# A Mamba-2 (SSD) mixer stage, reordered: the next group's projections stand between this group's heads, VectorE works on whole rows of chunks, and ScalarE and GpSimd split the weights

## The chip, the core and the metric

The kernel runs on one core of one Trainium2 chip. A core has five engines that run side by side and meet only at semaphores: TensorE (PE; its weight loads are listed apart as PEld), VectorE (DVE), ScalarE (ACT), GpSimd (POOL) and SyncE (SP), which here starts the DMAs. The metric is the device time of one execution in microseconds (us). Matmuls read SBUF and write PSUM (8 banks of 512 floats in each of 128 partitions).

## The reference

Two layers of a diffusion backbone run over 640 tokens: 512 latent tokens and 128 context tokens. Layer 0 mixes tokens with a bidirectional Mamba-2 scan, layer 1 with gated DeltaNet, and each is followed by an expert-retrieval mixer. The change touches the Mamba-2 mixer alone:

```python
proj = h @ w_in                                  # z, xbc, dt
xbc  = silu(short_conv(xbc, conv_w) + conv_b)    # 3 taps along the tokens
dt   = softplus(dt_raw + dt_bias);  a = -exp(a_log)
acs  = cumsum(dt * a)                            # inside a chunk
lmat = exp(where(tril, acs[i] - acs[j], -inf))   # decay matrix of a head
cb   = einsum('bcign,bcjgn->bcijg', cm, bm)      # C_i . B_j, one per group
y_in = einsum(cb * lmat, x * dt)                 # inside a chunk
y_x  = einsum(c, state) * exp(acs)               # from the states before it
s    = s * exp(acs[-1]) + einsum(b, xdt * exp(acs[-1] - acs))
y    = rmsnorm((y_f + y_b + xs * d_skip) * silu(z)) @ w_out
```

There are 4 groups of 8 heads; each head has 64 channels and a state of 128; every step is done forward and backward. The reference has chunks of 64 tokens, the kernel takes chunks of 128, so 4 latent chunks and 1 of context.

## The kernel before

Activations lie features-first: 128 features in the partitions, 640 tokens along the row. The stage in question is `ssd_groups_phase` (line 600), which loops over the 4 groups. A group has ten weight tiles of 128 columns: four of x, one of B, one of C (these six go through the conv) and four of z, the gate. Projections are fp32 in three passes: the weight and the input are each split into a high and a low part, and `project` (L673, matmuls at L187) does high x high, high x low and low x high, 48 matmuls of 320 columns for a tile. A weight tile lands in one buffer `w` (L666); VectorE rounds it to the high part (L339) and subtracts to get the low part (L341); TensorE waits for both.

Within a group the work goes in three steps:

- Conv tiles: TensorE projects six tiles in a row, ScalarE takes the middle tap (L756) and the SiLU (L760), VectorE adds the two outer taps out of PSUM (L427).
- States: TensorE turns x and B to tokens-first (L689) and makes `cb` (L695). VectorE weighs the tokens (L824), TensorE makes the eight state increments one by one (L703), and VectorE carries the states from chunk to chunk (L842, L847).
- Heads: for head r, `sums` (L712) makes the cumulated decay of both directions in PSUM. VectorE takes the difference with a mask added, chunk by chunk (L858), ScalarE takes two exponentials (L772, L773), VectorE multiplies by C (L887), by dt, adds the directions and multiplies by `cb` (L890, L895, L899), and TensorE multiplies the result `m` with the tokens and `ea` with the states (L735, L738). Every second head a z tile is projected first, and `heads_out` (L866, L871) writes two heads.

Each engine takes its instructions in the written order, and semaphores carry what one engine owes another. PSUM is four slots of two banks; a table (`order`, L609) says who uses which slot next. The loop over groups is one body, run four times: a group's first projection stands behind the last head of the group before, and VectorE lets the next group begin (`group_free`, L903) when its last output is written. TensorE's order inside the heads is these lines:

```python
for r in range(SR):
    if r + 1 < SR:
        sums(r + 1)
    ...
    if r % 2 == 0:
        project(SCONV + q)
        slots.claim(pe, ("y", q), i)
    ...
    pe.wait_ge(m_ready, SR * i + r + 1)
```

Of the kernel before, what the change touches and what calls it, by code (L numbers as in the profile page):

```python
# [16 lines left out]
ALU = mybir.AluOpType  # L17
# [416 lines left out]

def out_projection_phase(k, name, w_dram, src, tiles, layer):
# [164 lines left out]
def ssd_groups_phase(k, parts, stats, y):  # L600

    nc, d = k.nc, k.dram
    NW = 2
    assert STILES % NW == 0 and SXT > NW + 1
    FWD, BWD = 0, 1


    incs = [(FWD, 0), (BWD, 3), (FWD, 1), (BWD, 2), (FWD, 2), (BWD, 1), (FWD, CTXC), (BWD, CTXC)]
    order = [(("proj", t), t % 4) for t in range(SCONV)]  # L609
    order += [(("turn", c), (SCONV + c) % 4) for c in range(NC)]  # L610
    order += [("cb", 3)] + [(("inc", n), 2 + n % 2) for n in range(len(incs))]
    order += [((what, r), slot) for r in range(SR) for what, slot in (("sumf", 0), ("sumb", 1))]

    order += [((what, n + q), 2 + q % 2) for q in range(SXT) for what, n in (("proj", SCONV), ("y", 0))]
    with ExitStack() as ctx:
# [4 lines left out]
        convw_all, convw = sb("convw_all", [P, SG, SCONV, 4]), sb("convw", [P, SCONV, 4])  # L620
        skip_all, skip = sb("skip_all", [P, SG, SXT]), sb("skip", [P, SXT])
        st = sb("stats", [P, 5, NC, 2, SR])
        xbc = sb("xbc", [P, SCONV, T])
        tok = sb("tok", [P, NC, (SXT + 1) * P])
        cb = sb("cb", [P, T])
        state = sb("state", [P, 2, NC - 1, SXT * P])
        lm = sb("lm", [P, 2, 2, T])
        ea = sb("ea", [P, 2, 2, T])
        m = sb("m", [P, 2, T])

        tap = m
        xw = ea[:, 0].rearrange("p d t -> p (d t)")[:, 0:2 * SXT * P].rearrange("p (b n) -> p b n", b=2)
        decayed = ea[:, 1].rearrange("p d t -> p (d t)")[:, 0:SXT * P]
        ctx_state = lm[:, 1].rearrange("p d t -> p (d t)")[:, 0:2 * SXT * P].rearrange("p (b n) -> p b n", b=2)
        ysum = sb("ysum", [P, T])
        B, C = xbc[:, SXT], xbc[:, SXT + 1]

        small, w_loaded, w_split = sem("small_loaded"), sem("w_loaded"), sem("w_split")
        init_loaded, group_free, stat_ready = sem("init_loaded"), sem("group_free"), sem("stat_ready")
        centre, tapped, convolved, gated = sem("centre_ready"), sem("tapped"), sem("convolved"), sem("z_ready")  # L640
        turned, cb_ready = sem("turned"), sem("cb_ready")
        weighted, states_ready, ctx_ready, ctx_stored = (sem(s) for s in (
            "weighted", "states_ready", "ctx_ready", "ctx_stored"))
        diff, lm_ready, m_ready, m_used = sem("diff_ready"), sem("lm_ready"), sem("m_ready"), sem("m_used")
        ps = k.ps
        block = ctx.enter_context(nc.Block())

        @block.sync
        def _(sp):
            sp.dma_start(convw_all[:], d["ssd_conv"]).then_inc(small, 16)  # L650
            sp.dma_start(skip_all[:], d["ssd_skip"]).then_inc(small, 16)
            with sp.Fori(0, SG) as i:
                for t in range(STILES):
                    if t == SCONV:
                        sp.wait_ge(group_free, i + 1)
                        for dr, first in ((FWD, 0), (BWD, NC - 2)):
                            sp.dma_start(state[:, dr, first], d["ssd_state"][bass.ds(2 * i + dr, 1)]
                                         .rearrange("o n p -> n (o p)")).then_inc(init_loaded, 16)
                    if t == SCONV + NW + 1:

                        for dr in range(2):
                            sp.wait_ge(ctx_ready, 2 * i + dr + 1)
                            sp.dma_start(d["ssd_out"][bass.ds(2 * i + dr, 1)].rearrange("o n p -> n (o p)"),
                                         ctx_state[:, dr]).then_inc(ctx_stored, 16)
                    sp.wait_ge(w_split, STILES * i + t + 1)
                    sp.dma_start(w[:], d["ssd_w_in"][bass.ds(STILES * i + t, 1)]  # L666
                                 .rearrange("o p k n -> p (o k) n")).then_inc(w_loaded, 16)
            sp.wait_ge(ctx_stored, 32 * SG)

        @block.tensor  # L670
        def _(pe):
            with pe.Fori(0, SG) as i:
                def project(t):  # L673
                    pe.wait_ge(w_split, STILES * i + t + 2)
                    slots.claim(pe, ("proj", t), i)
                    s = slots.slot(("proj", t))
                    for kt in range(KT):
                        last = three_passes(nc, ps[:, s], (whi[:, t % NW, kt], wlo[:, t % NW, kt]),
                                            (parts[0][:, kt], parts[1][:, kt]), kt == 0, kt == KT - 1)
                    last.then_inc(slots.ready[s], 1)  # L680

                for t in range(SCONV):
                    project(t)
                pe.wait_ge(convolved, SCONV * (i + 1))
                for c in range(NC):
                    slots.claim(pe, ("turn", c), i)
                    s = slots.slot(("turn", c))
                    for t in range(SXT + 1):
                        last = nc.tensor.transpose(ps[:, s, t * P:(t + 1) * P], xbc[:, t, c * P:(c + 1) * P],  # L689
                                                   k.c("ident"))  # L690
# [1472 lines left out]
```

## Time and profile before

| | us |
|---|---|
| median of 3 runs | 6237.69 (6228.37 to 6243.76) |
| the profiled execution's own time | 6234.22 |
| its span in the trace | 6232.4 |
| the stage: first weight DMA issued to last VectorE end | 217.85 to 1051.26 |

Over the whole span the page gives

```profile
PE 4920.7 (79%) x27154; PEld 4314.5 (69%) x27154; DVE 4364.5 (70%) x7749; ACT 1670.4 (27%) x2016; POOL 1605.7 (26%) x1060
```

That is an average over stages with different limits. The page's map cuts the span into 40 slices of 156 us; the stage is in the second to seventh:

```profile
PE   6677676854689999997777777777854589999997
POOL 0000000011026667773000000000011016666774
PEclk7788888877569999998888988899977559999999
```

[...] In the stage TensorE is busy six to seven tenths at some eight tenths of its clock, and GpSimd does nothing. A wait is read as: who waited, who released it, how long.

### The profile page before, as it was taken

Reading aid. Unit: us, or ns where it says so; the run is one execution under the profiler, and the core shown is the slowest. Engines: PE = TensorE matmul, PEld = TensorE weight load, DVE = VectorE, ACT = ScalarE, POOL = GpSimd, SP = SyncE. Lnnn points to the kernel's source line nnn. Section 1 sums busy time; section 2 is a strip of 40 time slices with the busy share of each in tenths; the row PEclk is TensorE's granted clock in tenths of the full one; section 3 lists DMA queues with packets and bytes.
Section 4 is the critical chain, followed back from the end, with each engine's and each line's share of the span. In section 5 each row is a group of like instructions: output and inputs, shape, how many; then the busy total and the mean of one; then the engine's idle time right before and its main releaser. Section 6 shows DMA issues by size and latency. Waiting matters only on the chain. (4 is left out here: it accounts for less than half of the span.)

```text
span 6232.4 us, 77006 instructions
## 1 busy us (share of the span) xinstructions
PE 4920.7 (79%) x27154; PEld 4314.5 (69%) x27154; DVE 4364.5 (70%) x7749; ACT 1670.4 (27%) x2016; POOL 1605.7 (26%) x1060
## 2 busy tenths in 40 slices
PE   6677676854689999997777777777854589999997
PEld 2566665754469888996766666666844359988896
DVE  1555554379759999998455555565279759999997
ACT  0122222211343333332212211121211243333332
POOL 0000000011026667773000000000011016666774
PEclk7788888877569999998888988899977559999999
DMA  8100110110159999995000000000110159999996
GB/s 359 40 28 21 38 38 4 54 38 23 71 234 402 401 401 397 397 398 209 29 25 25 25 25 21 16 18 21 54 38 23 54 217 401 401 402 398 397 395 261
DMA packets 340323, 1059.27 MB, mean 170 GB/s; under 512 B 28272, under 2 KB 135024, under 8 KB 316656
## 3 DMA queue, kind: packets, MB, share of 16 engines
q1 hardware_dynamic: 192624, 519.24, 22.0%
q0 software_dynamic: 147456, 536.94, 21.9%
q8 instruction: 135, 2.21, 0.2%
q14 instruction: 108, 0.88, 0.0%
HBM read 998.92 MB, written 57.15 MB: 169 GB/s over the span
## 5 line engine op out<-in xcount | busy, mean ns | idle before, releaser
L1836 POOL DMA_INDIRECT dense_ring<-in_peer_u_rows,dense_eid x512 | 723.3, 1413 | 934.6 <-DVEq L1952 583.8
L1608 POOL TENSOR_TENSOR top_w_lo<-top_w,top_w_hi 128x1024 fp32r<-128x1024 f32 x32 | 96.1, 3021 | 3342.4 <-ACTq L1576 3342.4
L1836 POOL DMA_INDIRECT dense_ring<-in_peer_v_rows,dense_eid x512 | 786.1, 1535 | 290.6 <-DVE dense_acc L1993 189.0
L1850 PE MATMUL psum<-peer_in_hi,dense_u_hi 128*128 128x384 f32 x2048 | 690.1, 337 | 44.8 <-DVE dense_u_lo L1958 44.8
L1850 PE MATMUL psum<-peer_in_hi,dense_u_lo 128*128 128x384 f32 x2048 | 690.4, 337 | 0.0
L1850 PE MATMUL psum<-peer_in_lo,dense_u_hi 128*128 128x384 f32 x2048 | 688.8, 336 | 0.0
L1993 DVE SCALAR_TENSOR_TENSOR dense_acc<-dense_ring,dense_weight,dense_acc 128x1024 f32<-128x1024 f32 x508 | 640.0, 1280 | 0.0
L1861 PE MATMUL psum<-dense_v_hi,dense_a_hi 128*128 128x512 f32 x1536 | 604.5, 394 | 18.7 <-DVE dense_a_lo L1972 17.1
L1985 DVE SCALAR_TENSOR_TENSOR dense_ring<-dense_ring,peer_rows 128x1024 f32<-128x1024 f32 x512 | 614.7, 1219 | 0.0
L1861 PE MATMUL psum<-dense_v_hi,dense_a_lo 128*128 128x512 f32 x1536 | 603.5, 393 | 0.0
L1861 PE MATMUL psum<-dense_v_lo,dense_a_hi 128*128 128x512 f32 x1536 | 602.8, 392 | 0.0
L1850 PEld LDWEIGHTS psum<-peer_in_hi,dense_u_hi 128*128 128x128 f32 x2048 | 386.6, 189 | 55.5 <-DVE dense_u_lo L1958 45.7
L1916 ACT CAST dense_a_hi<-dense_gelu 128x384 fp32r<-128x384 f32 x256 | 131.7, 515 | 1058.8 <-DVE dense_gelu L1967 1058.8
L1977 DVE TENSOR_TENSOR dense_v_lo<-dense_v,dense_v_hi 128x1024 fp32r<-128x1024 f32 x256 | 312.6, 1221 | 127.2 <-ACT dense_v_hi L1911 127.0
L1850 PEld LDWEIGHTS psum<-peer_in_lo,dense_u_hi 128*128 128x128 f32 x2048 | 386.2, 189 | 9.8
L1850 PEld LDWEIGHTS psum<-peer_in_hi,dense_u_lo 128*128 128x128 f32 x2048 | 385.9, 188 | 0.0
L1861 PEld LDWEIGHTS psum<-dense_v_hi,dense_a_hi 128*128 128x128 f32 x1536 | 289.2, 188 | 89.1 <-issue 23.9
L1911 ACT CAST dense_v_hi<-dense_v 128x1024 fp32r<-128x1024 f32 x256 | 268.4, 1048 | 277.0 <-DMA dense_v<-in_peer_v_rows 276.7
L1713 PE MATMUL psum<-gate_high,gate_second 128*128 128x128 f16 x768 | 324.8, 423 | 17.0 <-DVEq L1768 17.0
L1861 PEld LDWEIGHTS psum<-dense_v_hi,dense_a_lo 128*128 128x128 f32 x1536 | 288.7, 188 | 61.1
L1861 PEld LDWEIGHTS psum<-dense_v_lo,dense_a_hi 128*128 128x128 f32 x1536 | 288.9, 188 | 54.4
L1714 PE MATMUL psum<-gate_low,gate_second 128*128 128x128 f16 x768 | 324.2, 422 | 0.0
(339 smaller groups left out, 10170.4 us busy)
## 6 DMA issues: line engine op xcount, KB each, us to landing
dense_u<-in_peer_u SPq DMA_DIRECT2D x128, 1024.0 KB, 21.6
dense_v<-in_peer_v_rows SPq DMA_DIRECT2D x128, 1024.0 KB, 20.1
mod_w<-in_w_mod SPq DMA_DIRECT2D x24, 2048.0 KB, 16.7
gate_matrix<-gate_stage SPq DMA_DIRECT2D x12, 4096.0 KB, 11.1
dense_g<-gate_matrix SPq DMA_DIRECT2D x128, 384.0 KB, 15.6
gdn_w<-in_gdn_w_in SPq DMA_DIRECT2D x48, 512.0 KB, 3.4
ssd_w<-in_ssd_w_in SPq DMA_DIRECT2D x40, 512.0 KB, 3.3
top_w<-in_peer_w_q SPq DMA_DIRECT2D x32, 512.0 KB, 3.8
```

The source lines that it names most:

```text
L1608: nc.gpsimd.tensor_tensor(wlo[:, s].rearrange("p k n -> p (k n)"), w[:, s].rearrange("p k n -> p (k n)"), whi[:, s].rearrange("p k n -> p ...
L1713: nc.tensor.matmul(o, second[:, j, :, u], high[:, j, :, u], start=True, stop=False)
L1714: last = nc.tensor.matmul(o, second[:, j, :, u], low[:, j, :, u], start=False, stop=True)
L1836: nc.gpsimd.indirect_dma_start(ring[:, m % RING], None, table, bass.IndirectOffsetOnAxis(ap=eid[:, j, slot:slot + 1], axis=0)).then_inc(ro ...
L1850: last = nc.tensor.matmul(score_bank(e), w[:, e, cut], parts[x][:, kt, 0:DT], start=kt == 0 and n == 0, stop=kt == KT - 1 and n == 2)
L1861: last = nc.tensor.matmul(ps[:, c, at], x[:, e, c * P:(c + 1) * P], w[:, e, at], start=first and n == 0, stop=end and n == 2)
L1911: nc.scalar.copy(vhi[:, e], v[:, b, e * D:(e + 1) * D]).then_inc(vhi_ready, 1)
L1916: nc.scalar.copy(ahi[:, e], h[:, e]).then_inc(ahi_ready, 1)
L1977: nc.vector.tensor_tensor(vlo[:, e], v[:, m // 2 % 2, e * D:(e + 1) * D], vhi[:, e].bitcast(F32), ALU.subtract).then_inc(v_split, 1)
L1985: nc.vector.scalar_tensor_tensor(row, row, 1.0, rows[:, j], ALU.mult, ALU.mult, accum_out=dots[:, j, slot:slot + 1]).then_inc(row_used, 1)
L1993: nc.vector.scalar_tensor_tensor(acc[:, j], row, by, acc[:, j], ALU.mult, ALU.add).then_inc(row_used, 1)
```

## The change

The stage is rewritten; nothing else is. In words:

- The loops are written out: one list `seq` of all 40 tiles sets the order of projections. The first group's six conv tiles come first. Then each group has a chain stretch (its first two z tiles, and the B tile of the next group) and a head stretch, where the heads 0 to 7 have in front of them: the next group's C tile, z tile 2, the next x0, z tile 3, the next x1, nothing, x2, x3. The last group has only its z tiles there.
- A tile is projected in two halves of 320 columns, each in one bank; three banks go round.
- ScalarE rounds the weights to the high part, GpSimd subtracts the low part. `w` is still one buffer.
- The decay matrix is one buffer `lm` for both directions, made in whole rows: one difference of 1280, a clamp at 0 (`min`), exp, one product with `cb`, which now carries the triangle masks, and one with dt. GpSimd adds the two directions and multiplies `ea` (now 512 tokens a direction, not 640) by C. The next head's difference waits for this head's addition (`m_ready`).
- `stats` and the conv weights are used where they lie; the copies at a group's start go.
- The stored context states lie in `m`, so the first two additions of a group wait until their DMA has ended (`ctx_stored`).

TensorE at the change of heads. Before (heads 0 and 1; L735 and L738 are a head's products, L712 the sums of the next):

```order
L738 MATMUL psum<-ssd_ea,ssd_state 64x128 x2
L735 MATMUL psum<-ssd_m,ssd_tok 64x128
L712 MATMUL psum<-consts,ssd_stats 128x128 x10
L735 MATMUL psum<-ssd_m,ssd_tok 64x128
L738 MATMUL psum<-ssd_ea,ssd_state 64x128 x2
```

Now (L806 and L809 are the products, L743 the sums, L731 a projection):

```order
L809 MATMUL psum<-ssd_ea,ssd_state 64x128 x2
L806 MATMUL psum<-ssd_m,ssd_tok 64x128
L743 MATMUL psum<-consts,ssd_stats_all 128x128 x10
L731 MATMUL psum<-mixer_in_hi,ssd_w_hi 128x320
L731 MATMUL psum<-mixer_in_lo,ssd_w_hi 128x320
L731 MATMUL psum<-mixer_in_hi,ssd_w_lo 128x320
```

A projection of 48 matmuls, whose first three rows are shown, now stands between the sums and the next head's products in every head but one, not in every second.

VectorE over a head and a pair's output. Before (from the product with C on):

```order
L887 TENSOR_TENSOR ssd_ea<-ssd_ea,ssd_xbc 128x1280
L890 TENSOR_SCALAR ssd_lm<-ssd_lm,ssd_stats 128x128 x5
L895 SCALAR_TENSOR_TENSOR ssd_m<-ssd_lm,ssd_stats 128x128 x5
L899 TENSOR_TENSOR ssd_m<-ssd_m,ssd_cb 128x640
L858 SCALAR_TENSOR_TENSOR ssd_lm<-psum,ssd_stats,consts 128x128 x10
L117 REGISTER_ALU
L866 SCALAR_TENSOR_TENSOR ssd_ysum<-ssd_xbc,ssd_skip,psum 128x640
L870 REGISTER_ALU
L871 ISA
L871 TENSOR_TENSOR ssd_y<-ssd_ysum,ssd_y 128x640
```

Now (from the difference on):

```order
L992 TENSOR_TENSOR ssd_lm<-psum,ssd_stats_all 128x1280
L996 TENSOR_SCALAR ssd_lm<-ssd_lm 128x1280
L1000 TENSOR_TENSOR ssd_lm<-ssd_lm,ssd_cb 128x1280
L1003 TENSOR_TENSOR ssd_lm<-ssd_lm,ssd_stats_all 128x1280
L1008 SCALAR_TENSOR_TENSOR ssd_xs<-ssd_xs,ssd_skip,psum 128x640
L1012 TENSOR_TENSOR ssd_y<-ssd_xs,ssd_y 128x640
```

The product with C and the addition have left VectorE, and the pieces by chunk (x5, x10) have become whole rows.

ScalarE over a gate and a head. Before:

```order
L780 ISA
L780 ACT_TABLE_LOAD
L780 ACTIVATE ssd_y<-psum 128x640
L768 REGISTER_ALU
L117 REGISTER_ALU
L772 ACT_TABLE_LOAD
L772 ACTIVATE ssd_ea<-psum 128x640 x2
L773 ACTIVATE ssd_lm<-ssd_lm 128x1280
```

Now, two heads (L819 rounds a weight tile, L828 and L838 are the conv of the next group, L845 the gate):

```order
L856 ACT_TABLE_LOAD
L856 ACTIVATE ssd_ea<-psum 128x1024
L819 CAST ssd_w_hi<-ssd_w 128x1024
L860 ACTIVATE ssd_lm<-ssd_lm 128x1280
L828 ACTIVATE ssd_y<-psum,ssd_convw 128x320 x2
L856 ACTIVATE ssd_ea<-psum 128x1024
L819 CAST ssd_w_hi<-ssd_w 128x1024
L860 ACTIVATE ssd_lm<-ssd_lm 128x1280
L838 ACT_TABLE_LOAD
L838 ACTIVATE ssd_xs<-ssd_y 128x640
L845 ACTIVATE ssd_y<-psum 128x320 x2
```

The weight's rounding and the next group's middle tap and SiLU have come between the exponentials.

The diff, cut to its core (what is removed stands in the listing above):

```diff
+    def chain_tiles(i):
+        return [(i, Z), (i, Z + 1)] + ([(i + 1, XB)] if i + 1 < SG else [])
+    def head_tiles(i):
+        following = [(i + 1, t) if i + 1 < SG else None for t in (XC, 0, 1, 2, 3)]
+        c, x0, x1, x2, x3 = following
+        return [c, (i, Z + 2), x0, (i, Z + 3), x1, None, x2, x3]
...
+    order = [((tile, half), (2 * n + half) % 3) for n, tile in enumerate(seq) for half in range(2)]
...
         @block.tensor
+            for tile in seq[:SCONV]:
+                project(tile)
+            for i in range(SG):
+                project((i, Z))
+                pe.wait_ge(convolved, SCONV * (i + 1))
...
+                last.then_inc(cb_made, 1)
+                project((i, Z + 1))
+                pe.wait_ge(turned, NC * (i + 1))
+                sums(i, 0)
+                for n in range(4):
+                    increment(i, n)
+                if i + 1 < SG:
+                    project((i + 1, XB))
+                for n in range(4, NI):
+                    increment(i, n)
+                for r, tile in enumerate(head_tiles(i)):
+                    n = SR * i + r
                     if r + 1 < SR:
+                        sums(i, r + 1)
                     if r == 0:
+                        pe.wait_ge(inc_used, NI * (i + 1))
                         pe.wait_ge(states_ready, i + 1)
...
+                    if tile is not None:
+                        project(tile)
+                    pe.wait_ge(ec_ready, n + 1)
+                    pe.wait_ge(m_ready, n + 1)
...
         @block.scalar
+            def high(n):
+                act.wait_ge(w_loaded, 16 * (n + 1))
...
+                nc.scalar.copy(whi[:, n % NW], w[:]).then_inc(hi_ready, 1)
...
+                for r, tile in enumerate(head_tiles(i)):
+                    if r + 1 < SR:
+                        decay_row(i, r + 1)
+                    if tile is not None and at[tile] + 1 < len(seq):
+                        high(at[tile] + 1)
+                    if r + 1 < SR:
+                        decay_matrix(i, r + 1)
...
+        @block.gpsimd
+            def low(n):
+                pool.wait_ge(hi_ready, n + 1)
...
+                nc.gpsimd.tensor_tensor(wlo[:, b].rearrange("p k n -> p (k n)"),
+                                        w[:].rearrange("p k n -> p (k n)"),
+                                        whi[:, b].rearrange("p k n -> p (k n)").bitcast(F32), ALU.subtract
+                                        ).then_inc(w_split, 1)
+            def times_c(i, r):
+                pool.wait_ge(ea_ready, SR * i + r + 1)
+                e = ea[:, r % 2]
+                nc.gpsimd.tensor_tensor(e, e, bcast(bc[:, i % 2, 1, 0:LAT], 1, [P, 2, LAT]), ALU.mult
+                                        ).then_inc(ec_ready, 1)
+            def add_directions(i, r):
+                pool.wait_ge(lm_ready, n + 1)
...
+                nc.gpsimd.tensor_tensor(m[:, r % 2], lm[:, FWD], lm[:, BWD], ALU.add).then_inc(m_ready, 1)
...
         @block.vector
+            def difference(i, r):
+                dve.wait_ge(ea_ready, n + 1)
+                if n:
+                    dve.wait_ge(m_ready, n)
+                nc.vector.tensor_tensor(lm[:].rearrange("p d (c j) -> p d c j", j=P),
+                                        sums_ps.rearrange("p d (c j) -> p d c j", j=P),
+                                        bcast(by_chunk(SACS, i, r), 3, [P, 2, NC, P]), ALU.subtract).then_inc(diff, 1)
+                dve.drain()
+                nc.vector.tensor_scalar(lm[:], lm[:], 0.0, None, ALU.min).then_inc(clamped, 1)
+            def weigh_matrix(i, r):
+                dve.wait_ge(lm_exp, SR * i + r + 1)
+                nc.vector.tensor_tensor(lm[:], lm[:], cb[:], ALU.mult)
+                dve.drain()
+                l4 = lm[:].rearrange("p d (c j) -> p d c j", j=P)
+                nc.vector.tensor_tensor(l4, l4, bcast(by_chunk(SDT, i, r), 3, [P, 2, NC, P]), ALU.mult
+                                        ).then_inc(lm_ready, 1)
...
+                for n in range(4):
+                    update(i, n)
+                    if n < 2:
+                        weigh(i, n + 4)
+                weigh_matrix(i, 0)
+                for n in range(4, NI):
+                    update(i, n)
+                    if n < 6:
+                        weigh(i, n + 2)
...
+                for r, tile in enumerate(head_tiles(i)):
                     if r + 1 < SR:
+                        difference(i, r + 1)
+                        weigh_matrix(i, r + 1)
+                    if tile is not None and tile[1] < SCONV:
+                        taps(tile)
+                    if r % 2:
+                        heads_out(i, r // 2)
```

## Rows read from the trace of the kernel before

**Rows 1.** Stretches (us): busy time and count by engine, then granted clock (PEclk), DMA:
```profile
217.85:1051.26 833.41, 598.62 (x3596) 555.25 (x3596) 454.50 (x1064) 192.12 (x220) 0.00 (x0) 0.85 0.09 31
429.31:638.12 208.81, 150.75 (x899) 139.72 (x899) 113.62 (x266) 48.02 (x55) 0.00 (x0) 0.84 0.09 31
440.00:479.00 39.00, 37.21 (x254) 36.95 (x252) 21.75 (x43) 9.83 (x12) 0.00 (x0) 1.00 0.25 86
345.00:363.00 18.00, 10.74 (x65) 10.41 (x66) 7.93 (x23) 5.76 (x7) 0.00 (x0) 0.72 0.00 0
```

**Rows 2.** Waits, 216 to 1240 us: waiter, releaser, total us, times, longest:
```profile
DVE ssd_lm L858 <- PE psum L712: 191.8, 36, 9.8
PE psum L735 <- DVEq L900: 123.3, 24, 6.5
```

**Rows 3.** TensorE timeline, first group: start us, us, instruction, [idle before, releaser]:
```profile
271.25 4.26 PE L689 MATMUL psum<-consts,ssd_xbc 128*128 128x128 f32 x25 [4.16 <-ACT ssd_xbc L760]
275.35 1.28 PE L695 MATMUL psum<-ssd_xbc 128*128 128x128 f32 x10
...
281.05 1.12 PE L703 MATMUL psum<-ssd_ea,ssd_tok 128*128 128x512 f32 x2 [0.85 <-DVE ssd_ea L824]
...
313.56 0.41 PE L735 MATMUL psum<-ssd_m,ssd_tok 128*64 128x128 f32 x2 [2.37 <-ACT ssd_y L780]
...
314.24 0.38 PE L735 MATMUL psum<-ssd_m,ssd_tok 128*64 128x128 f32 x2
...
314.89 0.58 PE L735 MATMUL psum<-ssd_m,ssd_tok 128*64 128x128 f32 x2
...
316.12 0.63 PE L735 MATMUL psum<-ssd_m,ssd_tok 128*64 128x128 f32 x2
...
359.30 0.69 PE L735 MATMUL psum<-ssd_m,ssd_tok 128*64 128x128 f32 x2 [6.44 <-DVEq L900]
...
364.16 2.47 PE L712 MATMUL psum<-consts,ssd_stats 128*128 128x128 f32 x20
```

**Rows 4.** Groups by shape, whole span: busy us, mean ns, then idle before:
```profile
L1911 ACT CAST dense_v_hi<-dense_v 128x1024 fp32r<-128x1024 f32 x256 | 268.4, 1048 | 277.0 <-DMA dense_v<-in_peer_v_rows 276.7
...
L887 DVE TENSOR_TENSOR ssd_ea<-ssd_ea,ssd_xbc 128x1280 f32<-128x1280 f32 x32 | 47.6, 1487 | 20.7 <-ACTq L774 18.8 <-issue 1.3
...
L773 ACT ACTIVATE ssd_lm<-ssd_lm 128x1280 f32<-128x1280 f32 x32 | 40.7, 1271 | 0.0
...
L339 DVE CAST ssd_w_hi<-ssd_w 128x1024 fp32r<-128x1024 f32 x40 | 27.7, 693 | 24.7 <-DMA ssd_w<-in_ssd_w_in 18.2 <-issue 6.5
...
L772 ACT ACT_TABLE_LOAD x20 | 25.7, 1283 | 88.7 <-DVE ssd_lm L858 84.9 <-issue 3.7
...
L824 DVE TENSOR_TENSOR ssd_ea<-ssd_tok,ssd_stats 128x512 f32<-128x512 f32 x32 | 21.7, 690 | 2.2
...
L764 ACT COPY ssd_tok<-psum 128x640 f32<-128x640 f32 x20 | 13.8, 692 | 8.5 <-PE psum L689 7.9
```

**Rows 5.** VectorE timeline, conv taps of two neighbouring tiles, first group:
```profile
239.89 2.34 DVE L427 SCALAR_TENSOR_TENSOR ssd_m<-psum,ssd_convw,ssd_m 128x320 f32<-128x320 f32 x6 [2.49 <-ACT ssd_m L756]
...
246.93 2.34 DVE L427 SCALAR_TENSOR_TENSOR ssd_m<-psum,ssd_convw,ssd_m 128x320 f32<-128x320 f32 x6 [2.49 <-ACT ssd_m L756]
```

**Rows 6.** GpSimd timeline in the later retrieval stage, two subtractions a row:
```profile
1266.02 4.66 POOL L1608 TENSOR_TENSOR top_w_lo<-top_w,top_w_hi 128x1024 fp32r<-128x1024 f32 x2 [1265.56 <-ACTq L1576]
...
1317.98 7.14 POOL L1608 TENSOR_TENSOR top_w_lo<-top_w,top_w_hi 128x1024 fp32r<-128x1024 f32 x2 [20.79 <-ACTq L1576]
```

**Rows 7.** VectorE timeline beside the second of these:
```profile
1317.85 1.49 DVE L1637 TENSOR_TENSOR top_hit<-top_placef,consts 128x1280 f32<-128x1280 f32 x1
1319.41 3.47 DVE L1642 TENSOR_TENSOR top_hit<-top_hit,top_indexf 128x1280 f32<-128x1280 f32 x1
```

**Rows 8.** DMA issues: count, KB each, median us to landing:
```profile
ssd_w<-in_ssd_w_in SPq DMA_DIRECT2D x40, 512.0 KB, 3.3
...
out_ssd_out<-ssd_lm SPq DMA_DIRECT2D x8, 256.0 KB, 2.0
```

More of the change, by code:

```diff
@@ L432, in conv_taps, with split_taps, add @@
     return add(-1, w2)
+def split_taps(nc, out, banks, w0, w2):
+    def add(shift, w):
+        for bank, base, lo, hi in ((0, 0, 0, BANKED), (1, BANKED, BANKED, LAT), (1, BANKED, LAT, T)):
+            a = lo + (shift < 0 and lo in STARTS)
+            b = hi - (shift > 0 and hi in ENDS)
+            to = out[:, a + shift:b + shift]
+            nc.vector.scalar_tensor_tensor(to, banks[bank][:, a - base:b - base], w, to, ALU.mult, ALU.add)
+    add(1, w0)
+    nc.vector.drain()
+    add(-1, w2)
 def out_projection_phase(k, name, w_dram, src, tiles, layer):
@@ L648, in _ @@
         @block.sync
         def _(sp):
[L650 to L667, printed above, removed]
@@ L671, in _, with project @@
         def _(pe):
[L672 to L676, printed above, removed]
+            def project(tile):
+                pe.wait_ge(w_split, at[tile] + 1)
+                b = at[tile] % NW
+                for half in range(2):
+                    slots.claim(pe, (tile, half))
+                    s = slots.slot((tile, half))
+                    cols = slice(half * BANKED, (half + 1) * BANKED)
@@ new lines, in silu, with gate @@
+            def silu(tile):
+                i, t = tile
+                n = conv_at[tile]
+                if t < SXT and i:
+                    act.wait_ge(heads_done, SXT * (i - 1) + t + 1)
+                act.wait_ge(tapped, n + 1)
+                nc.scalar.activation(conv_out(i, t), tap[:, n % 2], ACT.Silu).then_inc(convolved, 1)
+            def gate(tile):
+                i, t = tile
+                for half in range(2):
+                    slots.wait(act, (tile, half))
+                    s = slots.slot((tile, half))
+                    nc.scalar.activation(y_tile(i, t - Z)[:, half * BANKED:(half + 1) * BANKED], proj_ps[s],
+                                         ACT.Silu).then_inc(slots.free[s], 1)
+                act.drain()
+                act.sem_inc(gated, 1)
@@ new lines, in taps, with weigh @@
+            def taps(tile):
+                i, t = tile
+                n = conv_at[tile]
+                banks = [slots.slot((tile, half)) for half in range(2)]
+                dve.wait_ge(centre, 2 * n + 2)
+                split_taps(nc, tap[:, n % 2], [proj_ps[s] for s in banks], convw[:, i, t, 0:1], convw[:, i, t, 2:3])
+                dve.drain()
+                for s in banks:
+                    dve.sem_inc(slots.free[s], 1)
+                dve.sem_inc(tapped, 1)
+            def weigh(i, n):
+                dr, c = incs[n]
+                dve.wait_ge(turned, NC * i + c + 1)
+                if xw_after[n] is not None:
+                    dve.wait_ge(inc_made, NI * i + xw_after[n] + 1)
+                nc.vector.tensor_tensor(xw[n].rearrange("p (r q) -> p r q", q=SP_),
+                                        tok[:, c, 0:SXT * P].rearrange("p (r q) -> p r q", q=SP_),
+                                        bcast(stats[:, SW, c, heads(i, dr)], 2, [P, SR, SP_]), ALU.mult
+                                        ).then_inc(weighted, 1)
```

422 lines of the change are left out of this document (217 added, 205 removed).

## The prediction

> **What bounds the kernel now.** First the stretches. The stage takes 833.4 us, of which TensorE is busy 598.6, VectorE 454.5, ScalarE 192, GpSimd nothing, and TensorE's granted clock is 0.85 [rows 1]. The second of the four groups takes 208.8 us. No engine is full; the waits say why [rows 2]: TensorE stands 123 us before a head's products until VectorE has made `m` (24 waits), and VectorE stands 192 us until TensorE has made the next `sums`. The two work in turn: in the heads VectorE has no work of another head, TensorE has a projection for every second head only. The timeline shows the price twice [rows 3]: the products at 359.30 come after 6.44 us of idling, and behind such idling TensorE is slow: two chunks of a head's products start 0.68 and 0.65 us apart, the next 1.23 (314.89 to 316.12). [...] So this stage is bound by handing over, and each idle stretch is paid again in clock.
>
> **What TensorE has to do, at full clock.** A projection: 7.04 us, the distance of two tiles' conv taps where TensorE runs through [rows 5]. The sums of a head: 2.47, at 364.16 [rows 3]. A head's products: four chunks at 0.66 and the short context chunk 0.4, so 3.0 [rows 3]. Turning x and B, with `cb`: 4.3 + 1.3 = 5.6; a state increment 1.1 [rows 3]. None of it is removed. For the stage that is 40 x 7.04 + 32 x 5.47 + 4 x 5.6 + 32 x 1.1 = 514 us, a floor that only idling and clock lie above.
>
> **Heads with a projection.** TensorE now does sums 2.47, projection 7.04, products 3.0: 12.5 us a head. The others must fit beneath. VectorE: difference and the two products of 1280 at 1.49 each, the first out of PSUM, say 1.55; clamp of 1280, between 0.8 (rounding 1024 in 0.69 is faster than one element a step) and 1.49, I take 0.85; taps 2.34; output 1.7 every second head [rows 4, 5]: 8.6 us. ScalarE: exp of 1024 and of 1280, 1.05 and 1.27; weight rounding 1.05; middle tap, SiLU or gate about 0.7 each; two table loads of 1.28: 7.7 us [rows 4]. GpSimd: two operations of 1024 at 2.33, the pair at 1266.02 taking 4.66 [rows 6]. The addition of 640 is not in the trace: at least 1.46 (in proportion), at most 2.33; I take 1.5. Together 6.2.
>
> Does anything come late for TensorE? Counted from a head's start: sums done 2.5, table load and exp 4.9, difference 6.5, clamp 8.2 (it stands until GpSimd's product with C ends at 7.3), exp 9.6, the products with `cb` and dt 13.5 (GpSimd's weight subtraction holds VectorE until 10.5), addition 15.1. TensorE asks for that `m` at 12.5 + 9.5 = 22: 7 us to spare. The taps of this head's tile end at 16.1; their bank is wanted by the second half of the next projection at 18.4: 2.3 us to spare, the tightest place. The next weight tile is split by 10.5 and wanted at 15. So these heads cost 12.5 us and the products' waits go. Head 5 has no projection; there sums 7 wait for difference 6, and heads 5 and 6 together take 19.1. From the C projection to the end of head 7: 10 + 4 x 12.5 + 19.1 + 10 = 89 us.
>
> That GpSimd and VectorE hinder each other is in the trace: beside VectorE's products of 1280 the same two subtractions take 7.14 instead of 4.66, and one of the products 3.47 instead of 1.49 [rows 6, 7]. I have counted it above as one holding the other off for a whole operation. [...]
>
> **The chain stretch** (from the first z projection): 7.0, turning and `cb` 5.6, second z tile 7.0, sums 2.5: 22. Then TensorE waits for VectorE: load and exp 2.4, difference and clamp with GpSimd's product between 3.2, the first state update 1.5, a weighing and the second update 2.3, which frees the fourth increment at about 32; that ends at 33.7, and the B projection runs to 42 (1.5 of it for the half clock after the idling). The last four increments each wait for an update of 1.4 to 1.5: 48. The sums of head 1: 50.4, and 2.5 more for the clock: 53 us. A group is 53 + 89 = 142, against 208.8.
>
> **Start and end.** First projection 3.3 (DMA) + 1.05 + 2.33 + 0.3 after the first DMA's start [rows 4, 6, 8]; that is 7.0; it takes 8.5, 1.5 of it for the clock after idling; five more at 7.04 to 7.7, say 7.4 (a weight's rounding stands behind the SiLU of the tile before last): the first z tile starts at 52.5. The last group has no projections to hide behind but two: chain 46, state out 2.0 [rows 8] and addition 1.5, then the ring through the one `lm` (difference, clamp, exp, two products, addition, 0.7 for GpSimd and five handovers of 0.12): 9.4 for each of seven heads, 6 for the projections, 7 for the last head and its output: 128.
>
> **Sum.** 52.5 + 3 x 142 + 128 = 607 for 833.4: 226 us less. The profiled execution's own 6234.2 (span 6232.4) becomes 6008; the median of the runs is 3.5 above it: 6012, which I round to 6010. I cost the written-out loops at nothing: the four groups take 833.4, 208.4 in the mean, and the second 208.8 [rows 1], so the first one's fresh code delays nothing; TensorE's work covers the fetching, and without that cover a new body would cost what the trace does not show.
>
> **The rivals.**
> 1. *The heads go by VectorE and GpSimd.* The exclusion and the one `lm` line up: 6.2 + 4.3 (clamp, two products, half an output) + 4.3 (difference, taps, half an output) + 1.27 come to 16 us a head if nothing overlaps, and the taps free their bank too late. For: rows 6 and 7, and only 2.3 us to spare. [...] Price: up to 3.5 x 21 heads = 74, so 6030 to 6085.
> 2. *The waits for `m` stay* (the change doesn't do what its order says, because GpSimd is late with each addition): the 123 us of rows 2 return: 6130. Against: the 7 us to spare.
> 3. *Slower than before.* GpSimd's three operations in series with VectorE's ring, all at the hindered 3.57: 10.7 + difference, clamp, exp, products 6.7 + taps and output 3.2 + table loads 2.6 = 23 us a head, 10.5 more on each of 32: 6345. It decides from a head of 12.5 + 226/32 = 19.6 us. For: one buffer each of `w` and `lm`. Against: the ring needs one addition, not three operations, and GpSimd's unhindered pair is 4.66.
>
> **How the numbers follow.** Forecast 0.62, own range 5985 to 6035: the low end has no clock loss in the chains (16 us) and the shorter clamp and handovers; the high end has the clamp at 1.49, the addition at 2.33 and 5 us more in each chain. Rival 1 0.26, rival 2 0.07, rival 3 0.05, of which 0.01 ends within 0.3%, about 19 us, about what a measurement of this kernel can tell from no change. The range 5985 to 6085 takes in the forecast and rival 1. Faster 0.94, same 0.01, slower 0.05.
>
> **What would show it.** Right: TensorE near 9 tenths and a clock near 1.0 in the heads; heads 12.5 us apart; waits of products for `m` near zero outside the last group; groups of 142; GpSimd's operations lengthened but not waited for. The forecast is wrong if projections wait for their bank (taps late), if products wait for the addition, or if the chain stretch is well over 53.

## The result, and the profile after

The changed kernel takes 5963.8 us (5960.4 to 5965.6, 4 runs) against 6237.9: ratio 0.9561, 95% interval [0.9545, 0.9578], 274 us less. Forecast were 6010, 5985 to 6085, so the sign and the place were right, but the gain was a fifth larger than the 228 us of the forecast and 21 us beyond the range. The profiled execution takes 5960.4 for 6234.2. Its stretches (us, busy time and count by engine, granted clock, DMA) answer to [rows 1]; first the stage, then its first three groups, the last one, and the heads of the second group:

```profile
219.75:808.20 588.45, 527.73 (x3596) 484.24 (x3596) 356.88 (x400) 227.67 (x264) 234.44 (x104) 0.95 0.14 44
274.00:411.30 137.30, 128.77 (x899) 118.51 (x898) 91.54 (x104) 58.18 (x68) 59.18 (x26) 0.98 0.16 51
411.30:548.40 137.10, 128.58 (x900) 118.34 (x899) 91.09 (x101) 57.99 (x67) 59.15 (x26) 0.98 0.15 47
548.40:688.40 140.00, 130.53 (x900) 120.65 (x899) 89.47 (x101) 58.01 (x67) 59.71 (x26) 0.96 0.14 46
688.40:808.20 119.80, 94.17 (x613) 82.06 (x611) 73.46 (x67) 34.78 (x38) 39.65 (x19) 0.89 0.06 18
457.90:545.00 87.10, 85.01 (x639) 82.20 (x638) 63.09 (x62) 42.80 (x47) 49.27 (x22) 1.00 0.13 39
```

The stage went from 833.4 to 588.5. TensorE is now busy 85.0 of 87.1 us in the heads, at full clock (1.00). The granted clock is a share of the full one, and the traces record it at 1.00 or 0.50 only (0.50 at 360 to 362 us before, for one). The timeline of TensorE (as [rows 3]) shows a head beside a projection: its products, the sums (20 matmuls), then 48 matmuls of a projection, left out here, and the next products with no wait before them:

```profile
465.14 0.43 PE L806 MATMUL psum<-ssd_m,ssd_tok 128*64 128x128 f32 x2
...
467.81 0.38 PE L806 MATMUL psum<-ssd_m,ssd_tok 128*64 128x128 f32 x2
468.12 2.50 PE L743 MATMUL psum<-consts,ssd_stats_all 128*128 128x128 f32 x20
...
477.59 0.43 PE L806 MATMUL psum<-ssd_m,ssd_tok 128*64 128x128 f32 x2
```

465.14 to 477.59 is 12.45 us for a head; the forecast was 12.5. The waits of TensorE in the stage, which answer to [rows 2]:

```profile
PE psum L755 <- DVE ssd_state L984: 18.6, 9, 4.0
PE psum L806 <- POOL ssd_m L925: 14.8, 6, 6.6
PE psum L731 <- POOL ssd_w_lo L907: 14.6, 7, 11.3
...
PE psum L731 <- DVEq L955: 4.2, 3, 1.4
```

The 123 us of waits before products have become 14.8, all in the last group. Another 4.2 us are waits for the taps' bank, the place that the prediction called the tightest. What is left is mostly the chain stretch (L755) and the stage's first weights (11.3).

The stage gives 245 of the 273.8 us. Of the rest, 23.8 come from a stage that nobody edited: the GDN stage (first weight DMA to the first DMA of its output weights) took 1388.2 us and now takes 1364.4. Its instructions last as long as before; the turn from one head to the next is shorter. VectorE's timeline there, before, where "issue" is idling in which it waited for nothing the profile shows:

```profile
3165.67 0.83 DVE L1437 TENSOR_TENSOR gdn_y<-gdn_xi,gdn_y 128x640 f32 x1 [0.19 <-issue]
3169.82 0.21 DVE L1314 COPY gdn_stats<-gdn_stats_all 128x60 f32 x1 [3.33 <-issue]
...
3171.99 1.23 DVE L341 TENSOR_TENSOR gdn_w_lo<-gdn_w,gdn_w_hi 128x1024 fp32r<-128x1024 f32 x1 [0.97 <-issue]
```

and after, the same instructions of the same loop:

```profile
2918.05 0.83 DVE L1585 TENSOR_TENSOR gdn_y<-gdn_xi,gdn_y 128x640 f32 x1 [0.19 <-issue]
2919.58 0.21 DVE L1462 COPY gdn_stats<-gdn_stats_all 128x60 f32 x1 [0.71 <-DVEq L1586]
...
2920.87 1.23 DVE L341 TENSOR_TENSOR gdn_w_lo<-gdn_w,gdn_w_hi 128x1024 fp32r<-128x1024 f32 x1
```

From the start of the last output to the end of the first weight split is 7.55 us before and 4.05 after. TensorE waits for this split at the turn, 16.01 us before and 12.51 after:

```profile
3173.35 0.90 PE L187 MATMUL psum<-mixer_in_hi,gdn_w_hi 128*128 128x320 f32 x2 [16.01 <-DVE gdn_w_lo L341]
```

```profile
2922.23 0.90 PE L187 MATMUL psum<-mixer_in_hi,gdn_w_hi 128*128 128x320 f32 x2 [12.51 <-DVE gdn_w_lo L341]
```

The DMA queues of this stage (packets, MB, share) tell what VectorE did in the 3.33: before

```profile
q14 instruction: 39, 0.32, 0.1%
```

and after

```profile
q14 instruction: 3, 0.02, 0.0%
```

Queue q14, of the kind "instruction", moves packets of 8.2 KB (0.32 MB / 39), some five a head before and hardly any now; I read them as fetches of code, of VectorE's above all. One of them falls into the 3.33 us of idling (3166.6 to 3169.8 us, before):

```profile
q14 instruction: 1, 0.01, 1.0%
```

### The profile page after: what moved, and what is told of

Read it like the earlier page. It is cut to its first block and busy times, and to the rows that moved or that the text cites. A ratio compares the mean times of both kernels' runs of the same rounds, so it can differ in the third digit from the quotient of the medians.

```text
span 5958.7 us, 75917 instructions
## 1 busy us (share of the span) xinstructions
PE 4847.5 (81%) x27154; PEld 4245.5 (71%) x27154; DVE 4265.3 (72%) x7085; ACT 1709.2 (29%) x2060; POOL 1856.5 (31%) x1164
## 5 line engine op out<-in xcount | busy, mean ns | idle before, releaser
L1984 POOL DMA_INDIRECT dense_ring<-in_peer_v_rows,dense_eid x512 | 799.1, 1561 | 278.7 <-DVE dense_acc L2141 170.3
L187 PE MATMUL psum<-peer_in_hi,top_w_hi 128*128 128x320 f32 x512 | 132.7, 344 | 238.3 <-POOL top_w_lo L1756 238.3
```

Of the source, the lines that this page charges most:

```text
L187: last = nc.tensor.matmul(out[:, b], lhsT, rhs[:, b * BANKED:(b + 1) * BANKED], start=start and n == 0, stop=stop and n == 2)
L1984: nc.gpsimd.indirect_dma_start(ring[:, m % RING], None, table, bass.IndirectOffsetOnAxis(ap=eid[:, j, slot:slot + 1], axis=0)).then_inc(ro ...
```

## The experiments

The SSD stage times below run to the issue of the next DMA after the stage (the load of the norm's gain), 1 us past VectorE's last instruction: by this count the stage takes 834.5 us before and 589.5 after. Kernels in which the stage's code is the same differ in it by up to 2.6 us (831.9 and 834.5; 588.8 to 590.1).

**Where the loop's code lies.** Theory A: the GDN loop of VectorE, 331 instructions, lies 40 instructions further on within the blocks of 128 that a packet of 8.2 KB seems to bring (packets 123 to 132 instructions apart, see below the table), because VectorE's code ahead of it grew by 296 (two blocks of 128 and 40), and there it is fetched once. Rival B: the stage ahead, its clock or its length, is what matters. 40 instructions more on VectorE, ahead of a load that it waits for anyway, put the old kernel's loop in the new place; 88 more put the new kernel's back in the old one:

```
             dve.wait_ge(loaded, 48)        # small stage ahead of the GDN heads
+            for _n in range(40):           # 88 in the changed kernel
+                dve.sem_inc(filler, 1)
```

> The kernel before, with 40 semaphore increments more on VectorE in the small stage ahead of the GDN heads, where VectorE waits for a load anyway; nothing else changes, but VectorE's code of the GDN loop (331 instructions) and of all that follows lies 40 instructions later, where it lies in the changed kernel within an instruction block of 8 KB. Theory A (code placement: that the unchanged GDN stage was 23.8 us faster in the changed kernel comes from where VectorE's loop body lies in its instruction blocks): SSD stage unchanged at 833 us, GDN stage falls from 1388 to 1364, VectorE's instruction fetches inside the GDN heads go from 5 a head to none, the time falls by 24 to 30 us to about 6210. Rival B (the GDN stage follows the clock, the memory layout or the length of the SSD stage): 1388 and about 6238, unchanged.

> The changed kernel with 88 such increments in the same place, which brings VectorE's GDN loop back to its place of before within a block (40 + 88 = 128 instructions, one block of 8 KB). Theory A: SSD stage unchanged at 588, GDN stage rises from 1364 to 1388, five fetches a head return, the time rises by 24 to 30 us to about 5990. Rival B: 1364 and about 5964, unchanged.

Measured: 6209.1 us, ratio 0.996 [0.995, 0.997], GDN stage 1364.8; and 5989.9, GDN stage 1389.5. The turn in the old kernel with 40 more, and in the new one with 88 more:

```profile
3161.33 0.83 DVE L1440 TENSOR_TENSOR gdn_y<-gdn_xi,gdn_y 128x640 f32 x1 [0.19 <-issue]
3162.84 0.21 DVE L1317 COPY gdn_stats<-gdn_stats_all 128x60 f32 x1 [0.69 <-DVEq L1441]
```

```profile
2919.82 0.82 DVE L1588 TENSOR_TENSOR gdn_y<-gdn_xi,gdn_y 128x640 f32 x1 [0.19 <-issue]
2923.97 0.21 DVE L1465 COPY gdn_stats<-gdn_stats_all 128x60 f32 x1 [3.32 <-issue]
```

The idling goes and comes with the place alone. Every kernel of this study that keeps the loop falls on one of two sides; the first column is the place of the loop's first instruction in VectorE's program, counted modulo 128:

```
place  kernel                                   GDN stage us   packets of q14 in it
 55    before                                      1388.2           39
 55    changed, 88 more                            1389.5           39
 17    before, group loop written out              1382.6           38
 17    the same, table loads late                  1385.3           39
  7    changed, low halves on VectorE              1380.7           39
 95    changed                                     1364.4            3
 95    before, 40 more                             1364.8            3
 95    changed, conv tiles not beside the heads    1364.1            3
 95    changed, B's projection earlier             1364.3            3
 95    changed, clamp three times                  1364.4            3
 95    changed, table loads late                   1364.4            3
```

A is shown, B has fallen; that 17 and 7 would be bad places was on record before the first kernel of each ran. 331 instructions are 2.6 blocks, so the loop touches three or four, by its place. The count's 0 is not where a block begins: with the GDN heads written out (a kernel below) 16 of the 20 packets of q14 in the stage start when VectorE is at 64 to 70 of this count, one for every 123 to 132 of its instructions, and the other four go with ScalarE's. If a packet starts when a block has been used up, blocks begin near 66, and the loop touches three of them from 95 and four from 55, 17 and 7. That four are one too many is how I read the five packets a turn; what holds the blocks was not measured.

**What the group loop cost.** The old kernel's loop over the groups as a Python loop, on four engines:

```
-            with act.Fori(0, SG) as i:
+            for i in range(SG):
```

> The kernel before with its loop over the SSD groups written out on all four engines, instructions and order the same. If the loop's turns cost little (the prediction's view): SSD stage 833, within 5 us. If code fetching at the turn is a part of the 18.5 us by which the SSD stage came out under the forecast: 833 falls by 10 to 20 us. For the GDN stage theory A gives 1388 us again: VectorE's loop would begin in a place of its block from which it reaches over four blocks, as before. Rival B, if the loops of the stage ahead mattered: 1364.

Measured: 6184.7 us, ratio 0.992 [0.990, 0.993]; SSD stage 784.1, so 50 us less, where at most 20 had been expected. GDN stage 1382.6 with 38 packets, as A has it. ScalarE's timeline of the second group's first head tells what changed; looped:

```profile
507.41 1.28 ACT L772 ACT_TABLE_LOAD   x1 [20.69 <-DVE ssd_lm L858]
...
520.75 1.28 ACT L780 ACT_TABLE_LOAD   x1 [9.59 <-PE psum L187]
```

and written out:

```profile
495.03 1.28 ACT L772 ACT_TABLE_LOAD   x1 [19.24 <-PE psum L712]
497.69 1.30 ACT L772 ACTIVATE ssd_ea<-psum 128x640 f32<-128x640 f32 x2 [1.38 <-DVE ssd_lm L858]
...
500.23 1.28 ACT L780 ACT_TABLE_LOAD   x1
508.02 0.70 ACT L780 ACTIVATE ssd_y<-psum 128x640 f32<-128x640 f32 x1 [6.50 <-PE psum L187]
```

In the loop the load at 507.41 comes after 20.69 us of waiting for VectorE (L858), the one at 520.75 after 9.59 for the projection (L187). Written out, the load for the gate runs at 500.23, and ScalarE then waits 6.50 us for the projection with the table in place. The exponentials wait for two engines: there the load still comes after the sums (L712, 19.24 us at 495.03), but the 1.38 us for VectorE lie behind it. Over the whole stage ScalarE idles 244.6 us before its 16 gate loads (L780) in the loop, and 1.4 written out. The looped kernel has an instruction more at each gate, right ahead of the load, and the trace records the wait for the projection with it; of the written-out kernel it records that wait with the gate's ACTIVATE. The loop's two (minimum, median, maximum ns, first and last start):

```profile
L780 ACTq FUSED_REGOPS  x16: 55/58/60, 311.2 to 1032.5; - x16
L780 ACT ACT_TABLE_LOAD  x16: 1283/1283/1283, 311.3 to 1032.6; - x16
```

That holds for these waits and not for every one of the loop: before the four loads of the conv's SiLU (L760) ScalarE idles 0.1 us in all, looped and written out. Theory C: most of the 50 us is this, that in the loop the loads of 1.28 us stand behind the wait and so between what ScalarE waits for and its result. To move the loads back, an increment between wait and operation:

```
                     act.wait_ge(diff, SR * i + r + 1)
+                    act.sem_inc(between, 1)        # and the same ahead of the gate
```

> The kernel before with its group loop written out, and one semaphore increment on ScalarE between the wait and the operation, ahead of each head's exponentials (line 772) and of each gate (line 780). The written-out kernel's SSD stage was 784 us where the loop's was 834.5. [...] The increment puts the loads behind the waits again: four gate loads at 1.3 to 1.6 us and one exponential load at 1.3 a group on the path of TensorE, so 784 goes to 808 to 816. Rival (code fetching at the turns alone makes the 50 us): 784 stays, within 4 us.

Measured: SSD stage 816.7, time 6211.8. ScalarE idles 240.4 us before the gate loads, and of the 86.3 before the exponentials' loads 83.3 end with VectorE's difference (L861 here), as in the loop and not with the sums. So 32.6 of the 50 us come back when the table loads stand behind the waits again, just past the 808 to 816 that C allowed: C is shown. The other 18 were not taken apart. The same edit in the changed kernel, ahead of decay rows, SiLUs and gates:

> The changed kernel with one semaphore increment on ScalarE between the wait and the operation of each decay row, SiLU and gate, so that the table loads in front of these come after the waits, as the prediction counted them (2.4 us from a chain's sums to the end of the exponential, of which 1.28 is the load). Theory C: the load is back on the path of each chain stretch, 4 x 1.3 us, and where a head's decay row or SiLU is late for TensorE, which two or three heads of a group nearly are, some microseconds more: SSD stage 588 rises to between 594 and 606. Rival (ScalarE's loads lie beside other work in this kernel): 588 within 3 us. The GDN stage, whose VectorE code does not move, stays at 1364.

Measured in one run: SSD stage 599.6 for 589.5, GDN stage 1364.4. ScalarE idles 56.8 us before the loads of decay rows and SiLUs, for 10.7 in the changed kernel.

**The overlap by itself.** The conv projections of each group ahead of its own chain again, the rest of the change kept:

```
-        return [c, (i, Z + 2), x0, (i, Z + 3), x1, None, x2, x3]
+        return [None, (i, Z + 2), None, (i, Z + 3), None, None, None, None]
```

> The changed kernel with the conv projections of each group ahead of its own chain, none beside the heads of the group before (the z projections stay). VectorE's code keeps its length and place. What is left is the regrouped VectorE work, the split of the weights over ScalarE and GpSimd, and the written-out loop. Theory (heads without a projection go by the ring through `lm` at 9.0 to 9.6 us, TensorE idles again): start 54, four groups of about 118, three times 43 for six projections, so SSD stage about 652 and the time about 6028; of the 245 us of the stage the overlap is then worth some 64 and the rest of the change 180. Rival (the overlap is nearly all of the gain): SSD stage about 790, time about 6165. GDN stage by theory A 1364 in both.

Measured: 6042.4 us, ratio 0.969 [0.968, 0.971]; SSD stage:

```profile
222.50:890.40 667.90, 552.44 (x3596) 499.23 (x3596) 343.42 (x400) 214.19 (x252) 228.67 (x104) 0.90 0.12 39
```

The groups take 164 us, where the expectation had 118 + 43 = 161; its terms add up to 655 and not to the 652 that it gives, so the stage came out 13 us above them. The overlap is worth 78 us (667.9 to 589.5). Of the rest of the stage's gain, 50 us is what writing out the loop gave in the old kernel (834.5 to 784.1); the other 116 (784.1 to 667.9) are the remaining rewrite, above all VectorE's wider operations and the work moved to ScalarE and GpSimd, which no run takes apart.

**The split of the weights.** The low halves on VectorE, the subtraction otherwise the same:

```
-                nc.gpsimd.tensor_tensor(wlo[:, b].rearrange("p k n -> p (k n)"), ...
+                nc.vector.tensor_tensor(wlo[:, b].rearrange("p k n -> p (k n)"), ...
```

> The changed kernel with the low halves of the weights made on VectorE (1.23 us each) instead of GpSimd. VectorE's work in a head grows from about 8.6 to 9.8 us, and GpSimd's falls by one operation. Theory (a head with a projection is bound by TensorE at 12.5 us, VectorE and GpSimd have some microseconds to spare): heads stay 12.4 to 12.5 us apart, SSD stage 588 within 5 us. Rival (the heads go by VectorE and GpSimd in turn): 1.2 to 1.5 us more in each of 21 heads, SSD stage 613 to 620. By theory A the GDN stage is 1388 here, with some 39 fetches of VectorE's, since its loop begins 40 instructions further on, in a place of its block from which it reaches over four.

Measured: 5969.6 us; SSD stage

```profile
219.70:802.90 583.20, 527.38 (x3596) 484.35 (x3596) 383.27 (x440) 227.54 (x264) 128.15 (x64) 0.94 0.14 44
```

and GDN stage 1380.7 with 39 packets, 8 us under the 1388. It is 6 us faster in its own stage, so giving the low halves to GpSimd gained nothing; the total is higher because the loop behind the stage lies in a bad place, which costs 16. VectorE's busy time grew by 26 us, though it got 40 operations of 1.22 (49 us): its other operations take 22 us less with this work gone from GpSimd. The largest share is the product with `cb`; with the low halves on GpSimd and on VectorE it takes (busy us, mean ns, idle before)

```profile
L1000 DVE TENSOR_TENSOR ssd_lm<-ssd_lm,ssd_cb 128x1280 f32<-128x1280 f32 x32 | 60.8, 1900 | 37.8 <-ACT ssd_lm L860 37.5
```

```profile
L991 DVE TENSOR_TENSOR ssd_lm<-ssd_lm,ssd_cb 128x1280 f32<-128x1280 f32 x32 | 47.8, 1493 | 16.3 <-ACT ssd_lm L860 16.0
```

**How much room the heads have.** The clamp three times:

```
+                for _ in range(2):
+                    nc.vector.tensor_scalar(lm[:], lm[:], 0.0, None, ALU.min)
+                    dve.drain()
```

> The changed kernel with the clamp of the decay matrix done three times instead of once, so two VectorE operations of 1280 more in each head's ring (0.83 us each alone, 1.5 where GpSimd holds them off): 1.7 to 3.0 us more. It asks how much room the heads have. Theory (heads bound by TensorE, 2.3 us to spare at the taps' bank, 7 for the decay matrix): heads beside a projection go from 12.46 to between 12.5 and 13.2 us, and the seven bare heads of the last group, which go by the ring, by the full 1.7 to 3.0: SSD stage 588 to between 602 and 625. Rival (VectorE and GpSimd in turn already are the bound): 14.2 to 15.5 us a head everywhere, SSD stage 640 to 680. VectorE's GDN loop lies 128 instructions later, one whole block, so by theory A the GDN stage stays at 1364 with 3 fetches.

Measured in one run: 6027.5 us, SSD stage 650.8. That is a time of the rival's (640 to 680), but neither account of the heads held. In the first group the products of heads 2 to 4 stay 12.5 to 12.7 us apart, but those of heads 1, 6 and 7 come 15 to 16.4 after the ones before. The waits of TensorE in the second group (us, times, longest):

```profile
PE psum L731 <- DVEq L955: 6.6, 2, 4.5
...
PE psum L806 <- POOL ssd_m L925: 4.5, 1, 4.5
```

So heads 2 to 4 have the 2 us that the prediction gave the heads beside a projection, but others have none: in the changed kernel one head of each of three groups already waits up to 1.4 us for its bank.

**Filling the chain, and the GDN loop.** B's projection between the second and third increment, head 0's products with `cb` and dt behind the updates; and, in another kernel, the GDN heads written out:

```
-                for n in range(4):
+                for n in range(2):
                     increment(i, n)
                 if i + 1 < SG:
                     project((i + 1, XB))
```

> The changed kernel with the projection of the next group's B between the second and the third state increment instead of the fourth and the fifth, and the two products of head 0's decay matrix behind the last state update on VectorE. Theory: TensorE's wait of 4.0 us at the third increment and the half clock behind it (1.2 us) go in three groups, of which 1 to 2 us come back at the later increments: SSD stage 588.5 falls by 9 to 14 us, time about 5952, groups 133 to 134 instead of 137. Rival (VectorE's chain of updates is the bound of this stretch, and only the place of the waiting moves): 588 within 3 us.

> The changed kernel with the loop over the GDN heads written out on four engines (order the same; TensorE's code grows from 1.05 to 1.83 MB). What the SSD loop gave when written out (50 us over four groups, a part of it table loads behind waits) should be there in a smaller share, since only two of a head's six table loads stand behind a wait: theory, GDN stage 1364 falls to 1320 to 1345, time 5920 to 5945. Rival (fresh code must be fetched for every head and delays TensorE): 1364 or more, up to 1400.

Measured for the first: 5954.8 us, SSD stage 582.5, groups of 134.5 to 135.7. That is 7 us less, under the 9 to 14 expected: in the second group TensorE's waits for the states fell from 4.1 to 1.3 us, but those for the weighed tokens rose from 1.9 to 2.3 and those for the taps' bank from 1.4 to 2.5. Measured for the second: 5927.1, GDN stage 1323.7, 41 us less, near the low end of the theory's 1320 to 1345. Two of ScalarE's table loads there, with the idling before them (busy us, mean ns, idle), looped in the changed kernel:

```profile
L1389 ACT ACT_TABLE_LOAD x8 | 10.3, 1283 | 73.2 <-DVEq L1465 73.2
...
L1408 ACT ACT_TABLE_LOAD x8 | 10.3, 1283 | 20.0 <-PE psum L187 20.0
```

and written out, where the first is gone altogether and the second has 0.8 us of idling before its eight, for 20.0:

```profile
L1408 ACT ACT_TABLE_LOAD x8 | 10.3, 1283 | 0.8
```

These loads, two a head, are by themselves 16 x 1.28 = 21 of the 41 us, by my estimate; the rest was not taken apart.

**Together.** Low halves on VectorE, the earlier B projection and the GDN heads written out:

> The changed kernel with what the runs so far point to, together: low halves of the weights on VectorE, B's projection between the second and third increment with the updates ahead of head 0's decay products, and the GDN heads written out. If the three add (6, 7 and 41 us by their stages): SSD stage 575 to 579, GDN stage 1324, time about 5912, between 5905 and 5922. Rival (the weight work on VectorE delays the updates that the new order of the increments leans on): SSD stage 583 to 590, time about 5922 to 5928.

Measured: 5891.5 us (5889.5 to 5892.2), ratio to before 0.9439 [0.9424, 0.9455], 72 us under the changed kernel and below the 5905 to 5922 of the sum. The two stages:

```profile
220.10:786.20 566.10, 518.70 (x3596) 480.21 (x3596) 383.45 (x440) 227.54 (x264) 128.31 (x64) 0.97 0.14 46
2720.70:4038.30 1317.60, 1014.71 (x6744) 906.99 (x6744) 800.34 (x1328) 265.62 (x360) 0.00 (x0) 0.91 0.07 24
```

The SSD stage is 10 us better than the sum of the parts: B's taps now come ahead of head 0's products with `cb` and dt, which was changed as well, and the clock is 0.97; which of the two it is was not separated.

## Why the prediction was wrong

The forecast for the profiled execution was 6008, and it took 5960.4: some 47 us, of which 24 lie in the GDN stage, 18 in the rewritten stage and 5 elsewhere.

- *The failed step: "the profiled execution's own 6234.2 becomes 6008".* It let everything outside the stage stand still, and costed the written-out loops at nothing. The change moved VectorE's code, and with it the place of the GDN loop: 23.8 us, shown both ways. With the loop in its old place the changed kernel measures 5989.9, inside the range. The sentence "TensorE's work covers the fetching" spoke of the rewritten stage, and of TensorE as cover; the engine that stalled was VectorE, in another stage, at a turn where TensorE waits for it. Writing out was not free of effect in the edited stage either: in the old kernel it took 50 of 834.5 us.
- *The stage itself* took 588.5 for 607: its start 1.7 us more (54.2 for 52.5), three groups 11.6 less (414.4 for 426), the last group 8.2 less (119.8 for 128). The sum's 1.5 and 2.5 us for the clock are my estimates: no row gives them. The trace shows the half clock itself, 0.50 from 436.6 to 443.4 us in the second group's chain; what it cost there was not taken apart.
- *Table loads* are a part of this. The term "load and exp 2.4" after the sums was read from a looped kernel, where the load follows the wait (at 507.41, above); written out, the exponential of the second group's chain ends 1.1 us after the sums. The late-load kernel gives 10.1 us back in all, some 3.5 each before the first group, in three groups and in the last; it is one run, and what else shortened the chain stretch was not taken apart.
- *The last group.* The sum added 6 us for its two projections beside the ring, and 2 for the state's way out. The ring was right: from head 0's products at 735.9 to head 7's at 801.6 are 65.7 us, forecast 7 x 9.4 = 65.8, but both projections fit inside it. Another 2 us are gone ahead of head 0's products (47.5 for 49.5); whether that is the table load or the state's way out is open.
- Some 5 us lie in the first layer's experts and behind the GDN stage, 3 each, less 2 at the start. Kernels with the same place of the loop differ as much there (experts 1176.6 to 1181.7, the end 1849.0 to 1854.0), so they stay unexplained.

What was right: heads of 12.5, groups at 138 for 142 (the chain stretch 46.6 for 53), heads 5 and 6 together 17.9 for 19.1, the waits for `m` gone outside the last group. ScalarE's terms add up to 7.3 (or 8.0 with three of the 0.7), not 7.7, which changes nothing here. The clamp, too, was right: it lasts 0.83 at the least for the 0.85 taken, and in most heads it takes longer, 1.48 in the median, as the prediction had it. The durations of clamp and difference (minimum, median, maximum ns):

```profile
L996 DVE TENSOR_SCALAR ssd_lm<-ssd_lm x32: 827/1483/2881, 297.8 to 794.1; 128x1280 f32<-128x1280 f32 x32
```

```profile
L992 DVE TENSOR_TENSOR ssd_lm<-psum,ssd_stats_all x32: 1475/1492/1494, 296.2 to 792.5; 128x1280 f32<-128x1280 f32 x32
```

Such lengthening goes with GpSimd's work beside it, and not in every operation. Of the 32 products with `cb` (L1000) 15 meet no operation of GpSimd's and take 1.49 us, the other 17 take 2.22 to 2.28. The clamp at 475.10 takes 2.88 and ends at 477.98, after GpSimd's weight subtraction (474.88 to 477.30). The difference, with one operand in PSUM, runs beside an operation of GpSimd's in all 32 heads and takes 1.48 to 1.49 each time. Rival 1 lost all the same, because TensorE's 12.5 us cover the lengthening; in the three-clamp kernel three heads of a group no longer hold it. Rivals 2 and 3 found nothing: there is no wait for `m` outside the last group.

## What to carry to other kernels

A forecast of a change that alters the length of an engine's code is a forecast for every loop of that engine behind it (here 23.8 us in the GDN stage): look for "issue" idling at a loop's turn and count the instruction packets there. A short loop whose body waits, loads a table and computes may be worth writing out: here the SSD stage fell from 834.5 to 784.1 us, and 32.6 of these came back when the table loads stood behind the waits again. Moving work to an idle engine is not free where the one lengthens the other's operations: here 49 us of subtractions, done by GpSimd, leave VectorE only 26 us less busy.

## What the hardware showed that was not expected

- The same 331 instructions of a VectorE loop cost 3.3 us more a turn (1388.2 against 1364.8 us, seven turns) by where they lie in blocks of 8.2 KB. In the slower place 39 packets of q14 fall into the stage, in the faster one 3, and one of the 39 lies in the 3.33 us of idling at the turn that is shown. The packets of the other instruction queue are twice as large: 16.4 KB (q8: 70, 1.15 MB in that stage).
- An activation table load of 1.28 us stood behind the wait of its gate in the loop and ran before the wait ended written out: ScalarE idled 244.6 us before the old kernel's 16 gate loads, 1.4 us written out, and 240.4 with an increment between wait and gate. With the exponentials' loads that was 32.6 us in one stage.
